# Laying the narrow projection columns of an attention layer out by kind, in one wide product per token block

## The chip, the cores and the metric

The kernel runs on one NeuronCore of a Trainium2 chip. The metric is the device time of one execution in microseconds; lower is better. Kernels are compared by the median of several executions.

## The reference

The reference runs three network blocks one behind the other on a sequence of 256 tokens with 1024 features, in 32-bit floats. The change is in the third block, a hybrid layer. There one input projection `h = x @ w_in` gives the operands of four mixers. Cut to what matters:

```
h = x @ w_in
(q_n, kc, vc, ks, vs, kw, vw, g_n, q_m, k_m, v_m, conv_in, q_h, f_h, i_h, g_h) = jnp.split(h, split_points, axis=-1)
gates = jax.nn.sigmoid(g_n.reshape(B, S, NSA_HEADS, 3))
o_nsa = nsa_attention(q_n, kc, vc, ks, vs, kw, vw, gates, rel_tab[:NSA_HEADS])
```

For the NSA attention q_n has 256 columns; the keys and values of its three branches, kc and vc (compressed), ks and vs (selected), kw and vw (window), have 64 columns each, shared by the four heads; and g_n has 12 columns, three gates for each of four heads. q_m, k_m and v_m, 256 columns each, belong to the second attention (MoBA).

## The kernel before

**Weights.** All large weights reach the core as 440 units of 128 x 2048 floats (1 MB), laid out on the host by `lay_unit`, in the order in which TensorE asks for them (`unit`). For a 1024-row weight a unit holds 256 columns of eight row tiles (j = 0 to 7). SyncE's queue loads unit n into a ring of three buffers, as soon as unit n - 3 has been split (`sp_weights`, L323). ScalarE makes the high part of it (`hi`, L118, the tile `weights_hi`), VectorE the rest (`lo`, L313, `weights_lo`), both into two buffers in turn. So `hi` of unit n waits for its transfer and for TensorE to have finished unit n - 2, `lo` waits for `hi`, and TensorE's first matmul of the unit waits for `lo`. The numbers of the units follow from the program, and each engine's order is the order in which its own function calls `hi`, `lo`, the copies and the matmuls.

**Products.** Every product is made of three matmuls in fp32r, high by high and the two mixed ones (`mm3`, L105): 24 matmuls for the 1024 rows. In a feature-major product (`pe_tile`) the weights are the stationary operand and the 256 tokens move (256 columns); the result has features on its partitions. In a token-major product (`pe_tokens`, `pe_tile_tok`) 128 tokens are stationary and the weights move, as many columns as there are features. In the trace the form `128*64 128x256` is a stationary operand of 64 columns and 256 moving ones, `128*128 128x12` one of 128 columns and 12 moving ones. Results stand in PSUM banks; before it writes a bank, TensorE waits in `empty` for the copies out of it that were named when the bank was last taken.

**The stage.** `pe_attention3` runs these products in a row: the NSA queries (Q_N, unit 0 of this count); a unit of 256 columns from KV_C on, which holds kc, vc, ks and vs; a unit from KV_W on, which holds kw, vw, the gates, and columns that nobody reads there; and then the projections Q_M, K_M, V_M, CONV_A and CONV_G, a unit each, 48 matmuls of 256 columns each (two tiles). Out of the two NSA units TensorE makes

- kc and vc together, one feature-major tile of 24 matmuls (bank 2),
- ks, 24 matmuls with 64 stationary columns (bank 3, `pe_keys`),
- vs, a token-major product for each block of 128 tokens, 2 x 24 matmuls of 64 columns (banks 0 and 1, `pe_tokens`),
- kw, as ks (bank 2); vw, as vs (banks 0 and 1),
- the gates, 2 x 24 matmuls of 12 columns (banks 2 and 3).

ScalarE's `act_attention3` copies the compressed pair (`cmp_tokens`, four copies, waits `kv_c`), each value product (`v_sel_win`) and applies the sigmoid to the gates (`nsa_gates`, L2990, waits `nsa_tokens`), with two calls of `hi` among them. VectorE's `dve_attention3` copies the two key products (`k_sel_win`, L3027 and L3030) between calls of `lo`. All of Q_M's, K_M's and later tiles go into banks 0 and 1 in turn (a projection takes both banks before its first matmul), and ScalarE and VectorE share the copies out of them (L435, L488).

Behind the projections, `pe_mixers`, `act_mixers`, `dve_mixers` and GpSimd's `pool_attention3` run the attentions, a 31-tap convolution and a recurrent mixer. The NSA part of it reads `k_sel_win`, `v_sel_win` and `nsa_gates`.

The semaphore of a signal is found by its kind (`TOGETHER`, L20 on): the kinds of one list share one semaphore, and the values are counted in program order.

Of the kernel before, what the change touches and what calls it, by code (L numbers as in the profile page):

```python
# [12 lines left out]
P = 128  # L13
# [20 lines left out]
    "scalar_attention": ("dup", "nsa_took", "cmp_exp", "cmp_by_key", "cmp_hid", "conv_silu"),  # L34
# [291 lines left out]
def empty(k, pe, b, *marks):  # L326

    for m in k.emptied[b]:
        pe.wait_ge(*k.s.at(*m))
    k.emptied[b] = marks  # L330
    return k.bank[b]
# [2450 lines left out]

MOBA = ("moba",)
# [3 lines left out]
def pe_tokens(k, pe, ap, at, width, b, bank, n):  # L2787
    out = empty(k, pe, bank, ("nsa_took", n))[:, 0:width]
    for j in range(KT):
        i = mm3(pe, out, k.x[:, j, b * P:(b + 1) * P], ap[:, j, at:at + width], j == 0, j == KT - 1)  # L2790
    i.then_inc(*k.s.up("nsa_tokens", n))


def pe_keys(k, pe, ap, at, bank, n):
    out = empty(k, pe, bank, ("k_sw", n))[0:64, 0:S]
    for j in range(KT):
        i = mm3(pe, out, ap[:, j, at:at + 64], k.x[:, j, :], j == 0, j == KT - 1)
    i.then_inc(*k.s.up("nsa_keys", n))
# [6 lines left out]
def pe_attention3(k, pe):  # L2805
    pe_project(k, pe, ("qn",), [w3(Q_N)], took_both(("qn",)), split_mark(("in3",)))
    ap = unit(k, pe, *w3(KV_C))
    out = empty(k, pe, 2, ("dup", 1, 1))[:, 0:S]
    pe_tile(k, pe, ap, 0, k.x, out).then_inc(*k.s.up("kv_c"))
    pe_keys(k, pe, ap, 128, 3, 0)  # L2810
    for b in range(NB):
        pe_tokens(k, pe, ap, 192, 64, b, b, b)
    unit_done(k, "nsa_tokens", 1)
    ap = unit(k, pe, *w3(KV_W))
    pe_keys(k, pe, ap, 0, 2, 1)
    for b in range(NB):
        pe_tokens(k, pe, ap, 64, 64, b, b, 2 + b)
    for b in range(NB):
        pe_tokens(k, pe, ap, 128, 12, b, 2 + b, 4 + b)
    unit_done(k, "nsa_tokens", 5)  # L2820
# [22 lines left out]
def pe_nsa_scores(k, pe, n):  # L2843
# [3 lines left out]
        bias_call(k, 2 * pair + hd, qb)], True, (("nsa_took", 5), ("k_sw", 1)))  # L2847
# [123 lines left out]
def act_attention3(k, act):  # L2971
# [13 lines left out]
    for n, (b, dst) in enumerate(((0, k.v_sw[:, 0, 0, :]), (1, k.v_sw[:, 1, 0, :]), (0, k.v_sw[:, 0, 1, :]),  # L2985
                                  (1, k.v_sw[:, 1, 1, :]), (2, k.gates[:, 0, :]), (3, k.gates[:, 1, :]))):
        if n == 2:
            hi(k, act)
        act.wait_ge(*k.s.at("nsa_tokens", n))
        act.activation(dst, k.bank[b][:, 0:12 if n >= 4 else 64], ACT.Sigmoid if n >= 4 else ACT.Copy) \  # L2990
            .then_inc(*k.s.up("nsa_took", n))
# [912 lines left out]
```

## Time and profile before

| | us |
|---|---|
| median of 3 runs | 3101.13 |
| lowest, highest run | 3089.43, 3102.24 |
| span of the profiled execution (first to last instruction) | 3091.2 |
| TensorE's matmuls busy | 2956.2 (96%) |
| VectorE busy, ScalarE busy, GpSimd busy | 1719.5 (56%), 1434.4 (46%), 166.1 (5%) |
| mean granted TensorE clock over the span (1.00 is 2.4 GHz) | 0.976 |
| moved by DMA | 492.89 MB, mean 159 GB/s |

The profile gives its execution's span and no separate time for it; the span lies 1.8 us above the lowest of the three runs and 9.9 us below their median. The profile is read in this way: the busy shares tell which engine has least room; the chain that ended last follows the end of the program back from one releaser to the next; the waits name who held whom up; the timeline gives each instruction's start and length; and the table of stretches gives, for any stretch, each engine's busy time and the clock that TensorE was granted in it. Matmuls overlap in the timeline, so their pace is the distance between two starts and not the length of one.

### The profile page before, as it was taken

The page shows a single profiled execution, that of the slowest core. Times are in us where ns is not written, and L with a number is a line of the kernel's source. Part 1 is how long each engine was busy: PE and PEld are TensorE (multiplying, and loading weights), DVE is VectorE, ACT ScalarE, POOL GpSimd, SP SyncE. Part 2 cuts the span into 40 slices and gives each one's busy share as a digit, 9 for nine tenths or more (in the row PEclk, how much of TensorE's full clock was granted, in tenths as well). Part 3 has the DMA queues.
Part 4 walks back from the last instruction along what each step waited for, and adds up shares of the span by engine and source line. Part 5 has one row for each costly group of instructions (what it writes and reads, how often), then busy time and mean ns, then how long its engine had stood idle before and what let it go on. Part 6 is the DMA issues. An engine that isn't in the chain of part 4 may idle for free.

```text
span 3091.2 us, 53947 instructions
## 1 busy us (share of the span) xinstructions
PE 2956.2 (96%) x23720; PEld 2748.8 (89%) x23720; DVE 1719.5 (56%) x2029; ACT 1434.4 (46%) x1831; POOL 166.1 (5%) x197
## 2 busy tenths in 40 slices
PE   8999998999999998999999999999979999999998
PEld 8988898999998998999989899899869899886887
DVE  5454555545464555545555654555786554465555
ACT  4455655445455655444445444444541344344444
POOL 1000100000000110001000000000011000045000
PEclk9999999999999999999999999999989999889999
DMA  6553334554543334556454455555320255441453
GB/s 249 185 189 124 137 137 153 188 191 177 184 180 128 138 141 158 185 185 230 180 204 165 154 186 186 179 181 191 138 82 4 73 189 185 151 152 54 152 179 134
DMA packets 69394, 492.89 MB, mean 159 GB/s; under 512 B 7853, under 2 KB 9421, under 8 KB 10534
## 3 DMA queue, kind: packets, MB, share of 16 engines
q1 hardware_dynamic: 64224, 465.53, 41.7%
q10 hardware_dynamic: 4938, 23.92, 2.0%
q8 instruction: 188, 3.08, 0.4%
q14 instruction: 44, 0.36, 0.0%
HBM read 488.32 MB, written 1.06 MB: 158 GB/s over the span
## 4 chain that ended last, share of the span: by engine, by line
PE 84%; DVE 8%; ACT 5%; issue 2%; PEld 0%; DMA 0%; POOL 0%; ACTq 0%; PEldq 0%; DVEq 0%; SPq 0%; POOLq 0%
PE bank L105 54%; PE acc L105 29%; ACT weights_hi L118 2%; DVE weights_lo L313 2%; DVE tmp L673 1%; DVE h L666 1%; DVE h L681 1%; PEld acc L105 0%; DVE b_x_lo L505 0%; PE acc L1005 0%; DMA weight_ring<-in_weights 0%; DVE b_x_lo L733 0%; ACT tmp L1084 0%; ACT L1084 0%; ACT b_x_hi L118 0%
## 5 line engine op out<-in xcount | busy, mean ns | idle before, releaser
L313 DVE TENSOR_TENSOR weights_lo<-weight_ring,weights_hi 128x2048 fp32r<-128x2048 f32 x440 | 1010.7, 2297 | 933.8 <-ACT weights_hi L118 933.3
L105 PE MATMUL bank<-b_x_hi,weights_hi 128*128 128x256 f32 x3576 | 1015.2, 284 | 15.6 <-DVE b_x_lo L733 10.6
L118 ACT ACTIVATE weights_hi<-weight_ring 128x2048 fp32r<-128x2048 f32 x440 | 839.6, 1908 | 370.6 <-PE acc L105 355.4
L105 PE MATMUL bank<-b_x_hi,weights_lo 128*128 128x256 f32 x3576 | 1009.6, 282 | 0.0
L105 PE MATMUL bank<-b_x_lo,weights_hi 128*128 128x256 f32 x3576 | 1008.3, 282 | 0.0
L105 PEld LDWEIGHTS bank<-b_x_hi,weights_hi 128*128 128x128 f32 x3576 | 677.3, 189 | 28.5 <-issue 13.3
L105 PEld LDWEIGHTS bank<-b_x_lo,weights_hi 128*128 128x128 f32 x3576 | 677.8, 190 | 3.4
L105 PEld LDWEIGHTS bank<-b_x_hi,weights_lo 128*128 128x128 f32 x3576 | 676.6, 189 | 0.0
L105 PE MATMUL acc<-weights_hi,b_hidden_hi 128*128 128x512 f32 x832 | 329.7, 396 | 0.0
L105 PE MATMUL acc<-weights_hi,b_hidden_lo 128*128 128x512 f32 x832 | 328.2, 394 | 0.0
L105 PE MATMUL acc<-weights_lo,b_hidden_hi 128*128 128x512 f32 x832 | 327.3, 393 | 0.0
L118 ACT ACTIVATE b_hidden_hi<-act_gate 128x256 fp32r<-128x256 f32 x208 | 86.9, 418 | 341.2 <-DVE act_gate L890 313.6
L866 ACT ACTIVATE act_gate<-bank 128x256 f32<-128x256 f32 x176 | 67.6, 386 | 276.0 <-PE bank L105 275.9
L105 PEld LDWEIGHTS acc<-weights_hi,b_hidden_lo 128*128 128x128 f32 x832 | 156.5, 188 | 37.9
L105 PEld LDWEIGHTS acc<-weights_lo,b_hidden_hi 128*128 128x128 f32 x832 | 156.7, 188 | 32.7
L105 PEld LDWEIGHTS acc<-weights_hi,b_hidden_hi 128*128 128x128 f32 x832 | 156.5, 188 | 32.5 <-DVE weights_lo L313 0.4
L105 PE MATMUL bank<-weights_hi,b_x_hi 128*128 128x256 f32 (+2 forms) x528 | 154.3, 292 | 9.3 <-DVE weights_lo L313 7.6
L105 PE MATMUL bank<-weights_lo,b_x_hi 128*128 128x256 f32 (+2 forms) x528 | 153.8, 291 | 0.0
L105 PE MATMUL bank<-weights_hi,b_x_lo 128*128 128x256 f32 (+2 forms) x528 | 153.8, 291 | 0.0
L105 PE MATMUL acc<-b_x_hi,weights_hi 128*128 128x256 f32 x416 | 125.4, 301 | 15.5 <-ACT tmp L1084 10.3
L893 DVE TENSOR_TENSOR b_hidden_lo<-act_gate,b_hidden_hi 128x256 fp32r<-128x256 f32 x176 | 75.3, 428 | 85.2 <-ACT b_hidden_hi L118 85.2
L105 PE MATMUL acc<-b_x_hi,weights_lo 128*128 128x256 f32 x416 | 121.5, 292 | 0.0
(487 smaller groups left out, 3999.6 us busy)
## 6 DMA issues: line engine op xcount, KB each, us to landing
weight_ring<-in_weights SPq DMA_DIRECT2D x440, 1024.0 KB, 4.8
xn<-in_norm_rows ACTq DMA_DIRECT2D x14, 1024.0 KB, 4.7
sgu_bias_row<-in_sgu_rows ACTq DMA_DIRECT2D x1, 2048.0 KB, 10.9
sgu_norm_rows<-in_sgu_rows ACTq DMA_DIRECT2D x1, 2048.0 KB, 9.6
bias_hankel<-bias_scratch ACTq DMA_DIRECT2D x1, 1536.0 KB, 6.2
h<-in_x SPq DMA_DIRECT2D x2, 512.0 KB, 6.6
mem_norm<-in_memory SPq DMA_DIRECT2D x1, 1024.0 KB, 13.8
sgu_w_spatial<-in_sgu_w_spatial ACTq DMA_DIRECT2D x1, 1024.0 KB, 4.7
```

Of the source, the lines that this page charges most:

```text
L105: return pe.matmul(out, a, b, start=start, stop=stop, skip_group_check=True)
L118: return act.activation(out, in_, ACT.Copy, scale=scale)
L313: dve.tensor_tensor(k.w.lo[:, n % 2, :], k.ring[:, n % RING, :], k.w.hi[:, n % 2, :], ALU.subtract) \
L666: dve.scalar_tensor_tensor(out=h, in0=h, scalar=alpha / scale, in1=acc_of(k, b), op0=ALU.mult, op1=ALU.add, accum_out=stat(k, 0, b)).then_ ...
L673: dve.scalar_tensor_tensor(out=k.t[:, b], in0=k.h[:, b, :], scalar=stat(k, 1, b), in1=k.rows[:, 0], op0=ALU.add, op1=ALU.mult).then_inc(*k ...
L681: dve.scalar_tensor_tensor(out=half(k.h[:, b], i), in0=half(k.t[:, b], i), scalar=stat(k, 6, b), in1=half(k.rows[:, 1], i), op0=ALU.mult, ...
L866: act.activation(k.act_gate[:, c, :], k.bank[c][:, 0:S], ACT.Silu).then_inc(*k.s.up("silu", f, j, c))
L893: dve.tensor_tensor(k.hid.lo[:, j % 2, c, :], k.act_gate[:, c, :], k.hid.hi[:, j % 2, c, :], ALU.subtract) \
```

## The change

The columns of the two NSA units are laid out anew. The first unit (`FEATURE_PARTS`) holds kc, vc, ks, kw, all that is wanted feature-major: TensorE makes two tiles of 128 features from it, the compressed pair in bank 2 and both keys in bank 3. The second (`TOKEN_PARTS`) holds vs, vw and the gates, 64 + 64 + 12 = 140 columns: one token-major product of 140 columns for each block of tokens, block 0 in bank 0 and block 1 in bank 1. `lay_unit` puts the columns together on the host. The number of units stays at 440.

```diff
-    "scalar_attention": ("dup", "nsa_took", "cmp_exp", "cmp_by_key", "cmp_hid", "conv_silu"),
+    "scalar_attention": ("dup", "v_sw", "gates", "cmp_exp", "cmp_by_key", "cmp_hid", "conv_silu"),
...
+def w3_parts(*parts):
+
+    return ("parts", "w_in_3", 0, parts)
+
+
+FEATURE_PARTS = w3_parts((KV_C, 128), (KV_S, 64), (KV_W, 64))
+TOKEN_PARTS = w3_parts((KV_S + 64, 64), (KV_W + 64, 76))
+TOKENS_W = 140
...
-def pe_tokens(k, pe, ap, at, width, b, bank, n):
-    out = empty(k, pe, bank, ("nsa_took", n))[:, 0:width]
+def pe_tokens(k, pe, ap, b):
+    out = empty(k, pe, b, ("gates", b))[:, 0:TOKENS_W]
     for j in range(KT):
-        i = mm3(pe, out, k.x[:, j, b * P:(b + 1) * P], ap[:, j, at:at + width], j == 0, j == KT - 1)
-    i.then_inc(*k.s.up("nsa_tokens", n))
-
-
-def pe_keys(k, pe, ap, at, bank, n):
-    out = empty(k, pe, bank, ("k_sw", n))[0:64, 0:S]
-    for j in range(KT):
-        i = mm3(pe, out, ap[:, j, at:at + 64], k.x[:, j, :], j == 0, j == KT - 1)
-    i.then_inc(*k.s.up("nsa_keys", n))
+        i = mm3(pe, out, k.x[:, j, b * P:(b + 1) * P], ap[:, j, 0:TOKENS_W], j == 0, j == KT - 1)
+    i.then_inc(*k.s.up("nsa_tokens", b))
...
 def pe_attention3(k, pe):
     pe_project(k, pe, ("qn",), [w3(Q_N)], took_both(("qn",)), split_mark(("in3",)))
-    ap = unit(k, pe, *w3(KV_C))
-    out = empty(k, pe, 2, ("dup", 1, 1))[:, 0:S]
-    pe_tile(k, pe, ap, 0, k.x, out).then_inc(*k.s.up("kv_c"))
-    pe_keys(k, pe, ap, 128, 3, 0)
+    ap = unit(k, pe, *FEATURE_PARTS)
+    pe_tile(k, pe, ap, 0, k.x, empty(k, pe, 2, ("dup", 1, 1))[:, 0:S]).then_inc(*k.s.up("kv_c"))
+    pe_tile(k, pe, ap, 1, k.x, empty(k, pe, 3, ("k_sw", 1))[:, 0:S]).then_inc(*k.s.up("nsa_keys"))
+    unit_done(k, "nsa_keys")
+    ap = unit(k, pe, *TOKEN_PARTS)
     for b in range(NB):
-        pe_tokens(k, pe, ap, 192, 64, b, b, b)
+        pe_tokens(k, pe, ap, b)
     unit_done(k, "nsa_tokens", 1)
-    ap = unit(k, pe, *w3(KV_W))
-    pe_keys(k, pe, ap, 0, 2, 1)
-    for b in range(NB):
-        pe_tokens(k, pe, ap, 64, 64, b, b, 2 + b)
-    for b in range(NB):
-        pe_tokens(k, pe, ap, 128, 12, b, 2 + b, 4 + b)
-    unit_done(k, "nsa_tokens", 5)
...
-    for n, (b, dst) in enumerate(((0, k.v_sw[:, 0, 0, :]), (1, k.v_sw[:, 1, 0, :]), (0, k.v_sw[:, 0, 1, :]),
-                                  (1, k.v_sw[:, 1, 1, :]), (2, k.gates[:, 0, :]), (3, k.gates[:, 1, :]))):
-        if n == 2:
-            hi(k, act)
-        act.wait_ge(*k.s.at("nsa_tokens", n))
-        act.activation(dst, k.bank[b][:, 0:12 if n >= 4 else 64], ACT.Sigmoid if n >= 4 else ACT.Copy) \
-            .then_inc(*k.s.up("nsa_took", n))
+    hi(k, act)
+    for b in range(NB):
+        act.wait_ge(*k.s.at("nsa_tokens", b))
+        copy_act(act, flat2(k.v_sw[:, b, :, :]), k.bank[b][:, 0:P]).then_inc(*k.s.up("v_sw", b))
+        act.activation(k.gates[:, b, :], k.bank[b][:, P:TOKENS_W], ACT.Sigmoid).then_inc(*k.s.up("gates", b))
...
-    dve.wait_ge(*k.s.at("nsa_keys", 0))
-    dve.tensor_copy(k.k_sw[:, 0, :], k.bank[3][0:64, 0:S]).then_inc(*k.s.up("k_sw", 0))
+    dve.wait_ge(*k.s.at("nsa_keys"))
+    for e in range(2):
+        dve.tensor_copy(k.k_sw[:, e, :], k.bank[3][64 * e:64 * e + 64, 0:S]).then_inc(*k.s.up("k_sw", e))
     lo(k, dve)
-    dve.wait_ge(*k.s.at("nsa_keys", 1))
-    dve.tensor_copy(k.k_sw[:, 1, :], k.bank[2][0:64, 0:S]).then_inc(*k.s.up("k_sw", 1))
```

The two waits of the NSA scores on `nsa_took` 5 (TensorE in `pe_nsa_scores`, VectorE in `dve_mixers`) become waits on `gates` 1, and `lay_unit` learns the kind "parts", which joins the named column ranges.

On TensorE the place is the end of the NSA products and the first matmuls of Q_M (in brackets the semaphores that a row waits for: `s_w_lo` is that of the unit's low part, `s_scalar_attention` that of ScalarE's copies out of the banks). Before:

```order
L105 MATMUL bank3<-weights_hi,b3_x_hi 128x12
L105 MATMUL bank3<-weights_lo,b3_x_hi 128x12
L105 MATMUL bank3<-weights_hi,b3_x_lo 128x12
L105 MATMUL bank0<-b3_x_hi,weights_hi 128x256 [waits s_scalar_attention,s_w_lo]
L105 MATMUL bank0<-b3_x_lo,weights_hi 128x256
L105 MATMUL bank0<-b3_x_hi,weights_lo 128x256
```

With the change:

```order
L105 MATMUL bank1<-weights_hi,b3_x_hi 128x140
L105 MATMUL bank1<-weights_lo,b3_x_hi 128x140
L105 MATMUL bank1<-weights_hi,b3_x_lo 128x140
L105 MATMUL bank0<-b3_x_hi,weights_hi 128x256 [waits s_scalar_attention,s_w_lo]
L105 MATMUL bank0<-b3_x_lo,weights_hi 128x256
L105 MATMUL bank0<-b3_x_hi,weights_lo 128x256
```

Q_M's first matmul stands 120 matmuls earlier. Its wait on ScalarE is for the copies out of banks 0 and 1: before, those of the value products, with 48 gate matmuls since; now those of the product that has just ended.

On ScalarE the place is the same stage, between the copies of the compressed pair and Q_M's:

```order
 L118 ACTIVATE cmp_tokens<-bank 64x256 x4
-L2990 ACTIVATE v_sel_win<-bank 128x64 x2
-L118 ACTIVATE weights_hi<-weight_ring 128x2048
-L2990 ACTIVATE v_sel_win<-bank 128x64 x2
-L2990 ACT_TABLE_LOAD
-L2990 ACTIVATE nsa_gates<-bank 128x12 x2
+L118 ACTIVATE weights_hi<-weight_ring 128x2048
+L118 ACTIVATE v_sel_win<-bank 128x128
+L2986 ACT_TABLE_LOAD
+L2986 ACTIVATE nsa_gates<-bank 128x12
+L118 ACTIVATE v_sel_win<-bank 128x128
+L2986 ACTIVATE nsa_gates<-bank 128x12
```

Q_M's high part moves ahead of all value copies, the table load stands between the first copy and the first sigmoid, and the copy and the sigmoid of the second block stand behind the last matmul of the stage.

## Rows read from the trace of the kernel before

**Rows 1.** The page: busy shares, and the chain that ended last by engine

```profile
PE 2956.2 (96%) x23720; PEld 2748.8 (89%) x23720; DVE 1719.5 (56%) x2029; ACT 1434.4 (46%) x1831; POOL 166.1 (5%) x197
...
PE 84%; DVE 8%; ACT 5%; issue 2%; PEld 0%; DMA 0%; POOL 0%; ACTq 0%; PEldq 0%; DVEq 0%; SPq 0%; POOLq 0%
```

**Rows 2.** Stretches of the stage: length, busy by engine, clock, DMA share, GB/s

```profile
2675.88:2678.72 2.84, 2.84 (x26) 2.84 (x25) 1.05 (x3) 2.38 (x3) 0.00 (x0) 1.00 0.58 237
2678.72:2681.52 2.80, 2.80 (x26) 2.80 (x25) 1.86 (x1) 1.52 (x4) 0.00 (x0) 1.00 0.03 6
2681.52:2688.06 6.54, 6.54 (x50) 6.54 (x49) 0.42 (x1) 0.23 (x1) 0.00 (x0) 0.80 0.48 162
2688.06:2692.79 4.73, 4.73 (x26) 4.73 (x26) 2.29 (x1) 2.02 (x2) 0.00 (x0) 0.56 0.00 0
2692.79:2700.27 7.48, 7.48 (x51) 7.48 (x49) 0.42 (x1) 0.22 (x1) 0.00 (x0) 0.69 0.40 142
2700.27:2710.51 10.24, 10.24 (x50) 10.24 (x50) 0.00 (x0) 1.69 (x3) 0.00 (x0) 0.50 0.00 0
2710.51:2719.64 9.13, 8.46 (x49) 8.28 (x50) 3.35 (x5) 2.99 (x5) 0.00 (x0) 0.69 0.35 115
```

**Rows 3.** Timeline of TensorE in the first 64-column products: start, length, instruction

```profile
2681.40 0.28 PE L105 MATMUL bank<-b_x_hi,weights_lo 128*64 128x256 f32 x1
2681.52 0.20 PE L105 MATMUL bank<-weights_hi,b_x_hi 128*128 128x64 f32 x1
2681.55 0.28 PE L105 MATMUL bank<-weights_lo,b_x_hi 128*128 128x64 f32 x1
...
2685.34 0.34 PE L105 MATMUL bank<-weights_hi,b_x_lo 128*128 128x64 f32 x1
2685.50 0.40 PE L105 MATMUL bank<-weights_hi,b_x_hi 128*128 128x64 f32 x1
```

**Rows 4.** Timeline of TensorE, first and last matmul of Q_M, first of K_M

```profile
2710.51 0.56 PE L105 MATMUL bank<-b_x_hi,weights_hi 128*128 128x256 f32 x1
...
2718.70 0.28 PE L105 MATMUL bank<-b_x_hi,weights_lo 128*128 128x256 f32 x1
2719.64 0.36 PE L105 MATMUL bank<-b_x_hi,weights_hi 128*128 128x256 f32 x1 [0.67 <-DVE q_moba L488]
```

**Rows 5.** Timeline of ScalarE between the key and the query products

```profile
2678.92 1.59 ACT L118 ACTIVATE cmp_tokens<-bank 64x256 f32<-64x256 f32 x4 [0.66 <-PE bank L105]
2684.32 0.23 ACT L2990 ACTIVATE v_sel_win<-bank 128x64 f32<-128x64 f32 x1 [3.81 <-PE bank L105]
...
2700.73 1.28 ACT L2990 ACT_TABLE_LOAD   x1
...
2710.69 0.18 ACT L2990 ACTIVATE nsa_gates<-bank 128x12 f32<-128x12 f32 x1 [4.94 <-PE bank L105]
2710.77 1.90 ACT L118 ACTIVATE weights_hi<-weight_ring 128x2048 fp32r<-128x2048 f32 x1
```

**Rows 6.** ScalarE's copy of 128x256 out of a bank

```profile
L435 ACT ACTIVATE v_moba<-bank x1: 384/384/384, 2731.3 to 2731.3; 128x256 f32<-128x256 f32 x1
```

**Rows 7.** Timeline of VectorE in the same stage

```profile
2678.29 2.29 DVE L313 TENSOR_TENSOR weights_lo<-weight_ring,weights_hi 128x2048 fp32r<-128x2048 f32 x1 [1.79 <-ACT weights_hi L118]
2681.72 0.42 DVE L3027 COPY k_sel_win<-bank 64x256 f32<-64x256 f32 x1 [1.14 <-PE bank L105]
```

**Rows 8.** Weight ring from 2655 to 2740 us: count of transfers and their landing

```profile
L323 SPq DMA_DIRECT2D weight_ring<-in_weights x8: 327/328/328, 2658.6 to 2736.7; - x8
...
DMA to landing us min/median/max: 4.7/4.9/6.6
```

**Rows 9.** Stretches elsewhere, columns as in Rows 2

```profile
221.00:224.00 3.00, 2.04 (x18) 1.84 (x16) 2.96 (x3) 2.18 (x3) 0.00 (x0) 1.00 0.01 3
224.00:228.00 4.00, 3.37 (x28) 3.37 (x29) 3.39 (x4) 1.27 (x1) 0.00 (x0) 1.00 0.52 205
...
2740.00:2770.00 30.00, 30.00 (x207) 23.82 (x205) 24.86 (x42) 17.73 (x31) 22.22 (x17) 1.00 0.42 153
```

More of the change, by code:

```diff
@@ L2846, in pe_nsa_scores @@
         (k.qn[:, 2 * pair + hd, qb * P:(qb + 1) * P], k.k_sw[:, kind, 0:(qb + 1) * P]),
-        bias_call(k, 2 * pair + hd, qb)], True, (("nsa_took", 5), ("k_sw", 1)))
+        bias_call(k, 2 * pair + hd, qb)], True, (("gates", 1), ("k_sw", 1)))
 def pe_compress(k, pe, e, half):
@@ L3539, in dve_mixers @@
     lo(k, dve)
-    dve.wait_ge(*k.s.at("nsa_took", 5))
+    dve.wait_ge(*k.s.at("gates", 1))
     dve_max(k, dve, ("nsa", 0), 0)
@@ L3765, in lay_unit @@
     w = inputs[name][index]
-    if kind == "rows":
+    if kind == "parts":
+        part = np.concatenate([w[:, at:at + n] for at, n in start], axis=1)
+    elif kind == "rows":
         part = w[start:start + 256]
```

## The prediction

> **What bounds the kernel now.** I read the page first. TensorE has matmuls running in 96% of the span, and 84% of the chain that ended last is its own work [rows 1]. So time is saved where TensorE gets less to do or does it faster, and a step on another engine counts only if TensorE comes to wait for it.
>
> Next I cut the stage of the change into stretches at the first matmul of each product [rows 2]. In order they are the compressed pair (24 matmuls, 2.84 us), the selected keys (24, 2.80), the selected values (48 of 64 columns, 6.54), the window keys (24, 4.73), the window values (48 of 64, 7.48), the gates (48 of 12 columns, 10.24), and Q_M up to the first matmul of K_M (48, 9.13). From the selected keys to K_M's start that is 40.92 us, with TensorE busy for 40.25 of them. The reader is to see two things. A product with 12 columns costs no less than one with 256. And the clock is at 1.00 (2.4 GHz) in the first two rows, at 0.50 (1.2 GHz) in the gates, and between them in the others, although TensorE has no idle time from the selected keys to the gates.
>
> The timeline shows why narrow products are dear. At full clock the 64-column matmuls from 2681.55 to 2685.34 start 34 steps apart, 0.1115 us each [rows 3]; those with 256 columns take 2.84 / 24 = 0.118 [rows 2]. At half clock the step is 10.24 / 48 = 0.213 with 12 columns [rows 2]. The step thus hardly depends on the moving columns; the 128-column weight load that each matmul brings is the likely floor. The clock fell at about 2685.4, after 3.9 us of 64-column products [rows 3]; it was back within the window keys, fell again in the window values, and came back only inside Q_M.
>
> **The change on TensorE.** It takes out 216 matmuls and puts in 96: 120 fewer.
>
> - Keys. The second tile of the new feature unit replaces both key products. It is a full 128 x 256 tile, as the compressed pair is: 2.84 us [rows 2] for 2.80 + 4.73 = 7.53. Gain 4.69.
> - Values and gates. 48 matmuls of 140 columns replace 144, which took 6.54 + 7.48 + 10.24 = 24.26 us. No row has 140 columns, so the step is bounded by the nearest ones: 0.1115 (64 columns) below, 0.118 (256) above. I take 0.1115, because the stationary operand is the same, and because 64 columns stream in no more than 0.03 us (the second 64-column matmul starts that soon behind the first [rows 3]), so 140 should in about 0.065, below the step. To the start of the last matmul that makes 47 x 0.1115 = 5.24 us (5.55 by the upper end).
> - The wait that is new. Q_M takes banks 0 and 1. Before, they had been copied out while the gates ran; now bank 1 holds the product that has just ended, so the copy and the sigmoid are exposed. The pattern stands at the other end of Q_M: from its last matmul to K_M's first 0.94 us pass, with one copy of 0.43 in it (idle 0.67, released by that copy) [rows 4]. Here ScalarE has a copy of 128 x 128 and a sigmoid of 128 x 12 in its place. The sigmoid took 0.18 [rows 5], the copy lies between 0.23 for 64 columns [rows 5] and 0.38 for 256 [rows 6]; I take 0.28. So 0.94 - 0.43 + 0.28 + 0.18 = 0.97 us from the last narrow matmul to Q_M's first (0.92 to 1.07). The table load of 1.28 us [rows 5] stands behind the first block's copy, under the 24 matmuls (2.7 us) of the second block: 0.28 + 1.28 + 0.18 = 1.74, covered by 0.9. If it were not, up to 1.3 us would be added.
> - Q_M itself. Before it began at half clock and took 9.13 us to K_M's first matmul. If the clock stays up in front of it, it takes 47 x 0.118 + 0.94 = 6.50. Gain 2.63, not from fewer matmuls but from the clock.
>
> Sum after: 2.84 + 5.24 + 0.97 + 6.50 = 15.55 us for 40.92. **Gain 25.4 us.** At full clock throughout, the old stage would have taken 2 x 2.80 + 3 x 5.35 + 6.50 = 28.2 us (5.35 is 48 x 0.1115), so half of the gain, 12.8, is the clock, and 12.6 the 120 matmuls less the new wait.
>
> On the clock the Trainium skill (TensorE: Matmul & The Clock Gate, "The HAM clock gate") says that it follows how busy the array is and that gaps between bursts throttle it. The trace agrees only in part: here it fell with TensorE's matmuls back to back and no gap. By the page, 140-column products without a gap hold the clock, which is the forecast; by the trace that has to be weighed, below. The same page ("Back-to-back issue gap") gives about 81 ns per pair of load and matmul at 128 columns; by that the 140-column product would take 3.8 us and the gain would be 26.8. The trace has 0.1115 for even fewer columns, and that decides.
>
> **The other engines and queues.** The weight supply has to follow a faster TensorE.
>
> - The token unit. Its high part is made as before, its low part from 2678.29 to 2680.58 [rows 7]; TensorE will want it at 2678.72 + 2.84 = 2681.6. Margin 1.0 us, where it was 7.5.
> - Q_M's unit. Its `hi` is queued on ScalarE ahead of the value copies, and waits for the keys' last matmul. Then 1.90 [rows 5] and 2.29 [rows 7] make 4.2, plus about 0.2 of hand-overs, under 5.24 + 0.97 of TensorE. ScalarE is free again 1.9 us after the keys, and the first block ends 2.7 us after them: nothing behind that `hi` is late. VectorE's two key copies (0.42 each [rows 7]) stand ahead of `lo`, but within the 1.90 us in which it waits for `hi`.
> - K_M's unit. Its `hi` starts behind the last sigmoid, with 4.4 us to go for 6.5.
> - The ring. SyncE's queue has the same 440 transfers. In this stage 8 of them landed in 4.7 to 6.6 us [rows 8]. Each may take two units' time, 11 us or more, as in the full-clock stretches. Cost nothing; the cover is that prefetch.
> - ScalarE has two operations fewer, VectorE has the same two copies; neither is on the path but for the new wait.
>
> What is late next is again TensorE, in the bank hand-overs of 0.9 us between projections. All behind them is released relative to Q_M's start, so the gain should reach the end whole.
>
> **The number.** The sum is made in the profiled execution: span 3091.2 - 25.4 = 3065.8 us. Against the median of the three runs, 3101.13, which lies 9.9 us above that span, it gives 3075.7 us, 0.8% less. About 0.5% (15.5 us) is what a measurement of this kernel can tell from no change; the three runs alone spread over 12.8.
>
> **Rivals.**
>
> - *The clock falls in the 140-column product too.* For it: 64 columns back to back did not hold it [rows 3]. Against it: a stretch in which matmuls of 256 columns ran for only 2.04 us out of 3.00 and then waited kept 1.00, and so did what followed [rows 9]; the new product has no such hole. 140 columns lie between these rows, nearer the 256 by ratio. Price: falling as late as the 64-column one did, the second block runs at 0.213, 24 x 0.102 = 2.4 us, and Q_M begins at half clock as before, 2.6; all 48 at half clock, 4.9 + 2.6. Gain 18 to 20.4, time about 3082. A short fall through the new pause alone costs some 1.5 us and belongs to the forecast.
> - *The step grows with the columns below 256.* If the 0.1115 of 64 columns were set by these and not by the load, 140 would take 0.244: 6.4 us more, gain 19.0, time 3082. Against it: the 0.03 us in which 64 columns streamed [rows 3], and 12 columns at half clock were no faster than the load.
> - *The units come late.* The margin of 1.0 us at the token unit, or a transfer that is slow because 3 MB are fetched in half the time, makes TensorE wait. To bring the gain below 15.5 us it has to lose 9.9; a transfer would have to land some 10 us later than the slowest of the eight [rows 8]. Time 3086 to 3097.
> - *Slower than before: the clock stays down through the mixers.* If the new pause, or the shifted places of the later pauses, left TensorE at half clock, each 256-column matmul would take 0.095 us more. After 267 of them (57 us) the gain is gone; the projections and the next unit are 288. With 430, up to the middle of the mixers, the kernel is 15.5 us slower, 3117. Against it: full clock came back inside Q_M with the same kind of stream, and the 30 us from 2740 on are at 1.00 with attention steps in between [rows 9].
>
> **Chances.** Forecast 0.76, clock falls 0.11, step by columns 0.06, late units 0.05, slower 0.02. The first gives faster by over 0.5% in 93 of 100 measurements (the gain is 10 us above the bound, the runs scatter by up to 6 each way), the next two in about 70, late units none. Faster 0.76 x 0.93 + 0.17 x 0.7 = 0.83, slower 0.02, within 0.5% 0.15. The range holds the forecast with the spread of the runs below (3101.13 - 25.4 - 12), and above the two rivals at 3082 with 7 us of spread: 3064 to 3089.
>
> **What would show it.** In the changed kernel: 96 matmuls between Q_N and Q_M, 48 of them with 140 columns at steps of 0.11 to 0.12; granted clock 1.00 from the compressed pair to the end of Q_M; one idle time of TensorE of 0.7 to 0.95 us in front of Q_M, released by ScalarE's `nsa_gates`; no idle time in front of the 140-column product; 15 to 16 us from the second feature tile to K_M. Steps of 0.21, or 0.24, would name the first or second rival, a wait on `weights_lo` the third, a clock below 1.00 in the projections behind the fourth. If the stage gains 25 us and the span does not, the forecast is wrong in that the gain reaches the end.

## The result and the profile after

| | kernel before | changed kernel |
|---|---|---|
| median, beside the first comparison (4 runs each) | 3100.32 | 3076.78 |
| lowest and highest of these | 3089.43 to 3102.24 | 3064.85 to 3077.64 |
| median, second comparison (11 and 6 runs) | 3100.04 | 3075.63 |
| span of the profiled execution | 3091.2 | 3075.8 |

The ratio of the times is 0.9921 with a 95% interval of 0.9901 to 0.9941, and 0.9924 [0.9912, 0.9936] in the second comparison. Forecast were 3075.7 us and a range of 3064 to 3089; the time is 1.1 us above the forecast, faster by more than 0.5%.

On the page of the changed kernel (busy shares, the clock in 40 slices, the chain that ended last), which answers to [rows 1]:

```profile
PE 2941.0 (96%) x23600; PEld 2732.3 (89%) x23600; DVE 1718.2 (56%) x2029; ACT 1436.3 (47%) x1829; POOL 166.3 (5%) x197
...
PEclk9999999999999999999999999999979999998999
...
PE 84%; DVE 8%; ACT 5%; issue 2%; PEld 0%; DMA 0%; POOL 0%; PEldq 0%; ACTq 0%; DVEq 0%; SPq 0%; POOLq 0%
```

TensorE has 120 matmuls fewer and bounds the kernel as before. The stage itself, in three stretches cut at the first matmul of the second feature tile, of the 140-column products and of Q_M (columns as in [rows 2]; the first three columns behind the stretch are its length, TensorE's matmuls and its weight loads, and the clock follows GpSimd):

```profile
2686.50:2689.36 2.86, 2.86 (x27) 2.86 (x25) 1.86 (x1) 1.52 (x4) 0.00 (x0) 1.00 0.13 26
2689.36:2695.36 6.00, 5.47 (x50) 5.35 (x49) 3.13 (x3) 4.15 (x7) 0.00 (x0) 1.00 0.57 186
2695.36:2701.97 6.61, 5.93 (x49) 5.76 (x49) 3.27 (x5) 2.68 (x4) 0.00 (x0) 1.00 0.52 207
```

Together 15.47 us, where the five stretches from the selected keys to K_M's start took 40.92 in [rows 2]. The clock is at 1.00 (2.4 GHz) in all three; in [rows 2] it went down to 0.50. TensorE's timeline shows the steps, in the form of [rows 3] and [rows 4]:

```profile
2689.36 0.23 PE L105 MATMUL bank<-weights_hi,b_x_hi 128*128 128x140 f32 x1
2689.42 0.27 PE L105 MATMUL bank<-weights_lo,b_x_hi 128*128 128x140 f32 x1
...
2694.56 0.27 PE L105 MATMUL bank<-weights_hi,b_x_lo 128*128 128x140 f32 x1
2695.36 0.36 PE L105 MATMUL bank<-b_x_hi,weights_hi 128*128 128x256 f32 x1 [0.53 <-ACT nsa_gates L2986]
```

From the second to the last narrow matmul (2689.42 to 2694.56) 46 steps pass, 0.1117 us each; then 0.80 us to Q_M's first. ScalarE's timeline, in the place of [rows 5], shows what TensorE waits for there:

```profile
2692.19 0.28 ACT L118 ACTIVATE v_sel_win<-bank 128x128 f32<-128x128 f32 x1 [0.66 <-PE bank L105]
2692.49 1.28 ACT L2986 ACT_TABLE_LOAD   x1
2693.78 0.18 ACT L2986 ACTIVATE nsa_gates<-bank 128x12 f32<-128x12 f32 x1
2694.87 0.28 ACT L118 ACTIVATE v_sel_win<-bank 128x128 f32<-128x128 f32 x1 [0.91 <-PE bank L105]
2695.05 0.18 ACT L2986 ACTIVATE nsa_gates<-bank 128x12 f32<-128x12 f32 x1
```

The table load lies wholly under the second block's matmuls. In the last two rows the sigmoid starts 0.18 us behind the copy's start, not 0.28: the two overlap by 0.10.

**Where the rest is.** The stage gained 25.45 us, the two profiled spans differ by only 15.4. The other 10 are not in the change: both executions run the same instructions ahead of it, and there the changed one was 7.6 us later (the high part of the first unit that the change touches was begun on ScalarE at 2676.72 instead of 2669.13). One stretch of RWKV and its neighbours holds nearly all of that. Kernel before, between two weight units:

```profile
2197.58:2478.02 280.44, 253.81 (x4127) 235.57 (x4126) 184.60 (x279) 100.45 (x152) 25.31 (x17) 0.94 0.21 73
```

Changed kernel, between the same two units:

```profile
2199.02:2486.64 287.62, 262.39 (x4127) 243.21 (x4126) 184.62 (x279) 100.97 (x153) 25.26 (x17) 0.91 0.21 73
```

The same 4127 matmuls, 7.2 us more, and a clock of 0.91 instead of 0.94; it is the 7 in the clock's slices above, where the page of before has an 8. Behind the stage it is another 2.3 us. Here and below that part is counted from the start of V_M's weight unit on ScalarE, which falls together with K_M's first products, to the end of the span (the expectations call it the stage's last unit, or its token unit): 371.9 before, 374.2 after. Over the 14 profiled executions of this study the start of that first touched unit lies between 2666.1 and 2677.9 us, and for one and the same kernel (tokens alone, below) at 2668.4 and 2673.0. The profiled execution of the kernel before was also one of its quicker ones: in every run that has both numbers the time is 1.8 us above the span, so its 3091.2 stands for some 3093, 7 us below the median, while the changed kernel's (3077.64) is 0.9 above its own. So a single pair of spans cannot show a gain of 25 us to better than some 10. The medians, 23.5 and 24.4 us apart, show it better; their intervals still leave 18 to 31 us and 20 to 27 us.

### The profile page after: what moved, and what is told of

The parts are those of the page before. It is cut to its first block, busy times and chain, and to the rows that moved or that the text cites. A ratio compares the mean times of both kernels' runs of the same rounds, so it can differ in the third digit from the quotient of the medians.

```text
span 3075.8 us, 53704 instructions
## 1 busy us (share of the span) xinstructions
PE 2941.0 (96%) x23600; PEld 2732.3 (89%) x23600; DVE 1718.2 (56%) x2029; ACT 1436.3 (47%) x1829; POOL 166.3 (5%) x197
## 4 chain that ended last, share of the span: by engine, by line
PE 84%; DVE 8%; ACT 5%; issue 2%; PEld 0%; DMA 0%; POOL 0%; PEldq 0%; ACTq 0%; DVEq 0%; SPq 0%; POOLq 0%
PE bank L105 53%; PE acc L105 29%; DVE weights_lo L313 2%; ACT weights_hi L118 2%; DVE tmp L673 1%; DVE h L666 1%; DVE h L681 1%; PEld acc L105 0%; DVE b_x_lo L505 0%; PE acc L1005 0%; DMA weight_ring<-in_weights 0%; DVE b_x_lo L733 0%; DVE tmp L613 0%; ACT tmp L1084 0%; ACT b_x_hi L118 0%
## 5 line engine op out<-in xcount | busy, mean ns | idle before, releaser
L105 PE MATMUL bank<-weights_hi,b_x_hi 128*128 128x256 f32 (+1 forms) x496 | 143.1, 289 | 8.9 <-DVE weights_lo L313 7.7
L105 PE MATMUL bank<-weights_lo,b_x_hi 128*128 128x256 f32 (+1 forms) x496 | 142.4, 287 | 0.0
L105 PE MATMUL bank<-weights_hi,b_x_lo 128*128 128x256 f32 (+1 forms) x496 | 142.1, 286 | 0.0
## 6 DMA issues: line engine op xcount, KB each, us to landing
mem_norm<-in_memory SPq DMA_DIRECT2D x1, 1024.0 KB, 14.2
```

What stands on the lines that cost most here:

```text
L105: return pe.matmul(out, a, b, start=start, stop=stop, skip_group_check=True)
```

## Experiments

### Old instructions, only wider: the clock by itself

The kernel before, its 144 narrow matmuls each moving 256 columns instead of 64 or 12. The number and order of the matmuls, the waits, and the number and width of the copies stay; the copies read their 64 or 12 columns where these now stand in the bank.

```
-    out = empty(k, pe, bank, ("nsa_took", n))[:, 0:width]
+    out = empty(k, pe, bank, ("nsa_took", n))[:, 0:256]
...
-        ... ap[:, j, at:at + width], ...
+        ... ap[:, j, 0:256], ...
```

> The kernel before, but each of its six narrow token-major products moves all 256 columns of the unit; the copies take the columns they want. As many matmuls as before, more columns. My theory (half of the gain is the clock, and a step costs a weight load whatever the columns): the clock stays at 1.00 from the keys to the end of the MoBA queries; the stage from the selected keys to the first matmul of the MoBA keys takes 2 x 2.80 + 144 x 0.118 + 6.5 = 29.1 us instead of 40.92, so this kernel is about 12 us faster than the one before (ratio 0.996). Rival (the number of matmuls and their columns set the time, and the clock fell by chance of the place): the stage takes 41 us or more, ratio 1.000 or above.

Measured: 3084.86 us median of 5 runs against 3098.86 of 9, ratio 0.9952 [0.9939, 0.9966]. The stage in stretches (selected keys; selected values; window keys; window values and gates; Q_M up to K_M):

```profile
2686.15:2688.95 2.80, 2.80 (x27) 2.80 (x25) 1.86 (x1) 1.51 (x4) 0.00 (x0) 1.00 0.07 21
2688.95:2694.64 5.69, 5.69 (x51) 5.69 (x49) 0.42 (x1) 0.22 (x1) 0.00 (x0) 1.00 0.49 186
2694.64:2697.43 2.79, 2.79 (x26) 2.79 (x25) 0.53 (x1) 2.03 (x2) 0.00 (x0) 1.00 0.00 0
2697.43:2708.83 11.40, 11.40 (x98) 11.40 (x97) 2.09 (x2) 1.91 (x4) 0.00 (x0) 1.00 0.27 93
2708.83:2715.38 6.55, 5.88 (x51) 5.70 (x49) 3.37 (x5) 3.02 (x5) 0.00 (x0) 1.00 0.12 21
```

29.2 us instead of 40.92, as expected, with four to twenty-one times as many columns moved in each of these matmuls and not one matmul fewer. The half clock is gone from every row. So narrow moving operands are what took the clock away, and that alone was worth 11.7 us here. The fewer matmuls of the real change bring the rest.

### Each half of the change alone

First the keys alone: the new feature unit and its full second tile, and behind it the old six products of 64, 64 and 12 columns out of the token unit (their six copies on ScalarE come back too).

```
     unit_done(k, "nsa_keys")
     ap = unit(k, pe, *TOKEN_PARTS)
-    for b in range(NB):
-        pe_tokens(k, pe, ap, b)
+    for n, (at, w) in enumerate(((0, 64), (64, 64), (128, 12))):
+        for b in range(NB):
+            pe_tokens(k, pe, ap, at, w, b, 2 * (n == 2) + b, 2 * n + b)
```

> Only the keys' part of the change: both keys in one full tile; values and gates stay narrow products (64, 64 and 12 columns for each block), out of the token unit. Theory by parts added up: 4.7 us less than before, stage 36.2 us. Theory with the clock: the second key product is gone that brought the clock back between the value products, so 34 of the 144 narrow steps run at 0.1115 and 110 at 0.213, 27.2 us, and the MoBA queries begin at half clock, 9.1: stage 39 us (38 to 40), only 1.5 to 2 less than before.

One execution: 3097.2 us. Its stretches (key tile; 96 matmuls of 64 columns; 48 of 12; Q_M up to K_M):

```profile
2678.93:2681.79 2.86, 2.86 (x26) 2.86 (x25) 1.87 (x1) 1.52 (x4) 0.00 (x0) 1.00 0.03 9
2681.79:2698.12 16.33, 16.33 (x98) 16.33 (x97) 3.13 (x3) 2.58 (x4) 0.00 (x0) 0.63 0.37 128
2698.12:2708.36 10.24, 10.24 (x49) 10.24 (x50) 0.00 (x0) 1.69 (x3) 0.00 (x0) 0.50 0.01 2
2708.36:2717.26 8.90, 8.23 (x50) 8.05 (x50) 3.36 (x5) 2.99 (x5) 0.00 (x0) 0.71 0.36 118
```

38.33 us, inside the 38 to 40 of the theory with the clock and not the 36.2 of the parts added up. As a difference of rows the prediction's 4.69 for the keys was right (7.53 became 2.86), but 1.9 of it is the low clock of the window keys; the keys alone bring 2.6. The window keys had brought the clock back between two narrow products; without them the 96 products of 64 columns run at 0.63 on average.

Then the tokens alone: the 140-column product, with the keys as two products of 64 rows.

```
-    pe_tile(k, pe, ap, 1, k.x, empty(k, pe, 3, ("k_sw", 1))[:, 0:S]).then_inc(*k.s.up("nsa_keys"))
+    for n in range(2):
+        out = empty(k, pe, 3 if n == 0 else 2, ("k_sw", n))[0:64, 0:S]
+        for j in range(KT):
+            i = mm3(pe, out, ap[:, j, 128 + 64 * n:192 + 64 * n], k.x[:, j, :], j == 0, j == KT - 1)
+        i.then_inc(*k.s.up("nsa_keys", n))
```

> Only the tokens' part: one product of 140 columns for each block, but the two keys as two products with 64 stationary columns, 24 matmuls each. Expected: clock 1.00 throughout; stage as in the changed kernel (15.47 us) with 2 x 2.80 for the keys instead of 2.86: 18.2 us. If the gain of the parts did not depend on the clock, it would be 20.2 (15.47 + 4.7).

(VectorE's two key copies follow.) One execution: 3079.54 us. From the first key product to K_M 18.22 us, as expected (2678.125 to 2696.342): keys 5.60, tokens with the new pause 6.01, Q_M 6.61. The last two stretches:

```profile
2683.72:2689.73 6.01, 5.48 (x50) 5.36 (x49) 2.71 (x2) 4.15 (x7) 0.00 (x0) 1.00 0.16 41
2689.73:2696.34 6.61, 5.94 (x48) 5.76 (x49) 3.35 (x5) 2.67 (x4) 0.00 (x0) 1.00 0.54 207
```

So the tokens alone are worth 22.7 of the 25.45 us, and the keys 2.75 on top of them. Merging the values and gates is the change; the key tile is a small addition.

### The step of a product, by its columns

Two variants of the changed kernel. In the first, the 140 columns are taken as 128 and then 12, so each block has 48 matmuls:

```
-    for j in range(KT):
-        i = mm3(pe, out, ..., ap[:, j, 0:TOKENS_W], j == 0, j == KT - 1)
+    for at, to in ((0, P), (P, TOKENS_W)):
+        for j in range(KT):
+            i = mm3(pe, out[:, at:to], ..., ap[:, j, at:to], at + j == 0, j == KT - 1)
```

> The changed kernel with each 140-column product cut into one of 128 and one of 12 columns, in the same bank: 48 matmuls more. If the step is the weight load whatever the columns, and the clock holds, the token products take 96 x 0.1115 = 10.7 us instead of 5.2, at 12 columns as at 128. If the step followed the columns, the 12-column ones would take next to nothing, and the token products stay near 5.5 us. If the clock falls in the 12-column ones, their steps are 0.213 from there on, and the MoBA queries begin below full clock.

One execution: 3095.53 us. Stretches (128 columns and 12 of the first block, 128 and 12 of the second, Q_M up to K_M):

```profile
2687.19:2689.81 2.62, 2.62 (x26) 2.62 (x25) 1.26 (x3) 1.91 (x1) 0.00 (x0) 1.00 0.88 306
2689.81:2693.39 3.58, 3.58 (x27) 3.58 (x26) 1.88 (x1) 0.00 (x0) 0.00 (x0) 0.73 0.45 108
2693.39:2698.55 5.16, 5.16 (x26) 5.16 (x26) 0.00 (x0) 1.74 (x3) 0.00 (x0) 0.50 0.42 178
2698.55:2704.30 5.75, 5.22 (x25) 5.16 (x26) 0.00 (x0) 0.49 (x3) 0.00 (x0) 0.50 0.00 0
2704.30:2712.79 8.49, 7.82 (x49) 7.65 (x49) 3.35 (x5) 2.67 (x4) 0.00 (x0) 0.75 0.34 125
```

and TensorE's timeline at the change from 128 to 12 columns, still at full clock:

```profile
2689.81 0.22 PE L105 MATMUL bank<-weights_hi,b_x_hi 128*128 128x12 f32 x1
2689.90 0.25 PE L105 MATMUL bank<-weights_lo,b_x_hi 128*128 128x12 f32 x1
...
2691.24 0.25 PE L105 MATMUL bank<-weights_lo,b_x_hi 128*128 128x12 f32 x1
```

From 2689.90 to 2691.24 there are 12 steps of 0.112 us with 12 columns; with 128 columns the step is 2.62 / 24 = 0.109, at half clock 5.16 / 24 = 0.215. 12, 64, 128 and 140 columns cost the same. But 48 more matmuls of 12 columns cost not only their 5.4 us: the clock falls during the first 24, and the 128-column products behind them run at half clock too. The span from the token product to K_M is 25.6 us against 12.6.

In the second, the product moves 256 columns, 116 of them padding that nobody reads.

> The changed kernel with the token products 256 columns wide instead of 140 (116 columns of padding more, never read). If the step of a product is set by more than its columns, as the 0.1117 us at 140 and the 0.118 us at 256 columns say, 47 steps cost 0.3 us more and the stage is 15.7 to 15.9 us. If columns set it, 47 steps would grow by 256/140 to 9.6 us and the stage be 19.8. The clock stays at 1.00 in the stage in either case.

Stretches (the 256-column token product with its pause; Q_M up to K_M):

```profile
2678.62:2685.00 6.38, 5.85 (x50) 5.68 (x49) 3.13 (x3) 4.15 (x7) 0.00 (x0) 1.00 0.60 187
2685.00:2691.61 6.61, 5.94 (x48) 5.76 (x49) 3.26 (x5) 2.67 (x4) 0.00 (x0) 1.00 0.58 196
```

0.38 us more than with 140 columns. The one execution took 3064.58 us; that it is below the changed kernel's median is not the wider product but mostly the part ahead: the first touched unit was begun at 2666.1, the earliest of all and some 10 us before the changed kernel's. Another 2.4 to 2.7 us came behind the stage (371.5 against 373.9 and 374.2).

### What is left of the stage: the bank hand-overs

Q_M, K_M, CONV_A and CONV_G each take over both banks just after they were filled, and TensorE waits for the last copy out of them. (V_M takes its banks one at a time and shows no wait.) The first two waits stand above; the other two, in the second execution of the changed kernel:

```profile
2713.34 0.36 PE L105 MATMUL bank<-b_x_hi,weights_hi 128*128 128x256 f32 x1 [0.56 <-ACT v_moba L435]
2719.88 0.36 PE L105 MATMUL bank<-b_x_hi,weights_hi 128*128 128x256 f32 x1 [0.61 <-DVE conv_in L3035]
```

First only the token products are moved to banks 2 and 3:

```
-    out = empty(k, pe, b, ("gates", b))[:, 0:TOKENS_W]
+    out = empty(k, pe, 2 + b, ("gates", b))[:, 0:TOKENS_W]
```

> The changed kernel with the token products in banks 2 and 3, nothing else: only the pause ahead of Q_M's first tile goes, and the three behind it stay. Theory (a pause costs its own length): stage 14.8 to 15.0 us instead of 15.5, median 0.5 to 1 us below the changed kernel, under what three rounds can tell. Rival (each pause also costs clock later, since the four together gave 9 us in the medians where they measure 2.4): 2 us or more below the changed kernel.

3074.62 us median of 4 runs (3067.8, 3070.4, 3078.8, 3080.9), ratio to the kernel before 0.9935 [0.9913, 0.9958]. The token stretch falls from 6.00 to 5.31 us, the stage to 14.79, as expected. The pause is gone and gives 0.69 us, somewhat more than its idle time of 0.53: from the last narrow matmul's start to Q_M's first it had been 0.80 us, and is now 0.11, one step. In the time of the whole 0.7 us cannot show: the four runs lie in two pairs ten microseconds apart, and the changed kernel was not run beside them. So whether a pause also costs clock later, the rival, stays open here.

Then K_M's and CONV_A's tiles also go to banks 2 and 3, so that neighbours alternate throughout (the copies follow):

```
+SHIFT = {("km",): 2, ("conv_a",): 2}
+def bank_of(of, t):
+    return (t + SHIFT.get(of, 0)) % 4
...
-        outs = [empty(k, pe, t % 4, *taken(t))[:, 0:S] for t in (2 * n, 2 * n + 1)]
+        outs = [empty(k, pe, bank_of(of, t), *taken(t))[:, 0:S] for t in (2 * n, 2 * n + 1)]
```

> The token products go to banks 2 and 3 and K_M's and CONV_A's tiles to banks 2 and 3 too, so that no tile follows another into a bank that was just filled. In the changed kernel TensorE paused 0.53 us ahead of Q_M's first tile, and before Q_M's, K_M's and CONV_A's neighbours the kernel before showed pauses of 0.56 to 0.67 us. Theory (the pauses are what is left of the stage, and nothing else is waited for there): the stage is 14.8 us to Q_M's side plus the removed pause of 0.6 at K_M, 14.2 to 14.4 us in all instead of 15.5, and with the pauses behind K_M the whole is 2 to 3 us shorter than the changed kernel, ratio to it about 0.9992, near what five rounds can tell. Rival (the pauses are filled by a weight wait behind them: the ring lands Q_M's unit too late): stage 15.3 or more, a wait named on weights_lo or weights_hi in place of that on the evacuation.

3066.61 us median of 5 runs, ratio to the kernel before 0.9902 [0.9888, 0.9916], beside 0.9924 [0.9912, 0.9936] for the changed kernel on the same chip. Key tile, tokens and Q_M:

```profile
2687.07:2689.91 2.84, 2.84 (x27) 2.84 (x25) 1.85 (x1) 1.52 (x4) 0.00 (x0) 1.00 0.03 3
2689.91:2695.22 5.31, 5.31 (x50) 5.31 (x49) 3.14 (x3) 3.65 (x4) 0.00 (x0) 1.00 0.57 201
2695.22:2700.96 5.74, 5.74 (x51) 5.74 (x50) 2.63 (x2) 2.53 (x4) 0.00 (x0) 1.00 0.56 193
```

The stage is 13.89 us, 1.6 below the changed kernel's and below the 14.2 expected, and none of the pauses is left among TensorE's waits. No weight unit comes late in their place: the rival is out. In the kernels that have them the four measure 0.53 + 0.67 + 0.56 + 0.61 = 2.4 us of idle time. What they cost is more: from the first token matmul to the end of CONV_G it is 34.0 us without them (2689.91 to 2723.91) and 37.2 with them (2688.54 to 2725.75), 3.2 us. The medians differ by 9.0, more than the 2 to 3 expected, yet the two intervals overlap, so how much of that is real stays open. In the profiled executions the part behind the stage went from 373.9 to 367.8 us, with 26.8 us at half clock instead of 33.8: some 3.5 us of it would be that.

### A wait in the mixers that some executions meet

The two experiments with 381.7 and 381.3 us behind the stage (tokens alone, and gates apart) had one thing in common: in the mixers TensorE reached the convolution's mean before GpSimd's last tap. To test it, that one step is moved in TensorE's order, behind the scores of head pair 3:

```
-    pe_conv_sum(k, pe, k.conv, ("mean", CONV), ...)
     pe_nsa_values(k, pe, ("nsa", 0), 0, 0)
     pe_nsa_scores(k, pe, 3)
+    pe_conv_sum(k, pe, k.conv, ("mean", CONV), ...)
```

It was made in the changed kernel first, then on top of the banks:

> The changed kernel once more, on the chip and beside the runs of the kernel before that the next three share. The stage from the first selected-key or pair product to the first K_M product should again take 15.5 us (between 15.3 and 15.7), wherever the span ends. The span itself may move by ten microseconds: the theory of the scatter is that in some executions TensorE reaches the convolution's mean before GpSimd's taps are done, waits about 0.9 us and then has the half clock for some 20 us, which costs about 10. If that theory holds, an execution of about 3075 us shows no wait on conv_out ahead of the mean, and one of about 3080 or more, if it is longer behind the stage, shows one.

> The changed kernel with one step of TensorE's order moved: the convolution's mean stands behind the scores of head pair 3 instead of ahead of the values of head pair 0. Theory (a wait for GpSimd's taps there, then 20 us at the half clock, makes the longer executions): the profiled execution shows no wait on conv_out ahead of the mean, and the stretch from the stage's token unit to the end is 372 to 375 us, never 378 or more; the median is up to 4 us below the changed kernel's if its executions fall on both sides, and equal where they mostly don't meet the wait. Rival (the wait is a symptom; the clock falls for another reason, the share of TensorE's work in that stretch): the half-clock stretch of about 20 us comes back in some executions without any wait ahead of it, and medians agree within 1 us. Second rival: VectorE, which centres after the mean, is now late for the maxima of head pair 3, and the time is up by 3 to 6 us.

> Both edits together. If they are independent, their gains against the changed kernel add: 2 to 3 us for the pauses, and 0 to 4 for the mean. If removing the pauses only brings TensorE earlier to GpSimd's taps (theory of the scatter), no_handover alone gives back part of its gain and this one does not: this one is then 3 us or more below no_handover.

The changed kernel again gave 3075.63 us (stage 15.46), with the mean later 3072.07 (6 runs, ratio 0.9916 [0.9901, 0.993]), with banks and mean 3070.43 (5 runs, 0.9907 [0.9895, 0.992]). For the theory these decide nothing: neither of the changed kernel's two profiled executions met the wait, so there was nothing to remove, and both are within each other's intervals. But they are a control: the move by itself leaves the part behind the stage as it was (374.2 us, beside 374.2 and 373.9). On top of the banks the step gains nothing (3070.43 against 3066.61), contrary to the expectation. In the kernel without pauses GpSimd's last tap came sooner too, 95.8 us after the start of V_M's weight unit, and TensorE at 97.4 did not have to wait for it.

The kernel with the tokens alone does meet it, so the step was tried there:

> The kernel of the token-products-only experiment again. Its stage should again be 18.2 us. Its one execution before had TensorE waiting 0.9 us for GpSimd's taps ahead of the convolution's mean and then 20.5 us at the half clock, and 381.7 us from the stage's last unit to the end against 371.9 to 374.2 in kernels without that wait. Theory (the wait brings the half clock on): if the wait is there again the part behind is 380 to 383 us, if not 372 to 375. Rival (chance, unrelated to the wait): the two come apart.

> The same kernel with the convolution's mean behind the scores of head pair 3, so that TensorE can't wait for GpSimd's taps there. Theory (the wait brings the half clock on): no wait, no stretch of 20 us at half clock, the part behind the stage 372 to 375 us, and the median 5 to 9 us below the kernel it is made from, where that one meets the wait in most executions. Rival (the half clock has another cause): the part behind is 380 us or more in spite of the missing wait, and the medians agree within 2 us.

Without the move 3082.67 us median (4 runs, 3080.14 to 3085.2; ratio 0.9962 [0.9947, 0.9977]), with it 3075.35 (4 runs, 3073.32 to 3077.43; 0.9937 [0.992, 0.9953]): 7.3 us, and no run of one among those of the other. Without the move the wait is there again, in TensorE's timeline:

```profile
2798.47 0.60 PE L105 MATMUL acc<-conv_out,cons 128*128 128x256 f32 x2
2799.94 0.70 PE L105 MATMUL acc<-conv_out,cons 128*128 128x256 f32 x2 [0.87 <-POOL conv_out L3129]
```

in GpSimd's, the last tap that it waits for:

```profile
2799.08 0.81 POOL L3129 TENSOR_TENSOR conv_out<-conv_out,conv_gate 128x256 f32<-128x256 f32 x1
```

and its stretches around that place:

```profile
2790.00:2800.00 10.00, 9.13 (x36) 4.69 (x33) 4.43 (x10) 5.43 (x15) 8.98 (x11) 1.00 0.09 37
2800.00:2810.00 10.00, 10.00 (x28) 5.22 (x28) 5.04 (x15) 1.54 (x5) 2.38 (x3) 0.63 0.01 2
2810.00:2820.00 10.00, 10.00 (x37) 6.56 (x37) 4.08 (x17) 3.78 (x16) 0.00 (x0) 0.69 0.00 0
```

With the move, the same stretches:

```profile
2790.00:2800.00 10.00, 10.00 (x44) 5.55 (x42) 4.03 (x10) 4.53 (x11) 8.92 (x12) 1.00 0.07 28
2800.00:2810.00 10.00, 10.00 (x48) 6.28 (x46) 6.52 (x19) 2.74 (x13) 2.48 (x3) 1.00 0.01 2
2810.00:2820.00 10.00, 9.29 (x38) 5.55 (x37) 3.48 (x16) 5.88 (x20) 1.78 (x3) 0.83 0.00 0
```

The wait is 0.9 us, but behind it the clock is at 0.63 and 0.69 for 20 us, and without it at 1.00 and 0.83. The part behind the stage is 378.0 us with the wait (the expectation had 380 to 383, so it was 2 us too high) and 374.2 without (372 to 375 expected). So the profiled pair shows 3.8 us for the wait; the rest of the 7.3 in the medians is not in this pair and was not traced.

Counted from the start of V_M's weight unit, GpSimd's last tap starts at 98.0 to 98.4 us in the twelve profiled executions of kernels whose K_M and CONV_A stand in their old banks. TensorE came to the mean 97.5 to 97.8 us after that point in the four that waited (377.8 to 381.7 us behind the stage). It came at 98.2 to 99.9 in the six with the mean in its old place that did not wait (371.5 to 374.2, and 378.5 for the keys alone). In all four that waited a stretch of 10.2 or 20.5 us at half clock begins at 101.6 to 102.0; none of the other ten executions has any half clock between 92 and 111. Nor does the early arrival by itself bring it on: in the kernel without pauses TensorE came at 97.4, found the taps done and kept its clock there. So the half clock that begins there goes with the wait. It is not the only way to a long part behind the stage: the keys alone have 378.5 without waiting, with 10.2 us at half clock from 122.9 on. A TensorE that came up to 2.3 us sooner to that place ended 4 to 10 us later, as far as these executions show.

Of the bank experiment's two pairs of runs, the profiled run (3080.93) is one that waits. Whether the lower pair escapes the wait or was quicker ahead of the stage, no trace shows.

## Why the prediction was right

- **Keys, 2.84 us.** Measured 2.86. The gain of 4.69 booked for them is in part the clock's, as the keys alone showed.
- **Token product, 47 x 0.1115 = 5.24.** Measured 5.20; the second matmul started 0.06 us behind the first, as estimated, and the other 46 steps are 0.1117. The rival "step grows with the columns" is out: 12, 128 and 140 columns have the same step, 256 has 0.118.
- **New wait, 0.97 (0.92 to 1.07).** Measured 0.80, outside its bounds: the one term that was clearly mis-sized. The copy's 0.28 and the sigmoid's 0.18 were right, but were added end to end. Their starts are 0.18 apart, an overlap of 0.10. The Trainium skill (ScalarE: Activation LUTs, "What ACT_TABLE_LOAD costs") says that back-to-back activations overlap by about 93 ns; the rows agree. The remaining 0.07 is the hand-over, 0.51 taken from the other end of Q_M, here 0.44. There, in the kernel before, the copy that [rows 4] name is

```profile
2719.01 0.43 DVE L488 TENSOR_SCALAR q_moba<-bank 64x256 f32<-64x256 f32 x1 [2.57 <-PE bank L105]
```

From the last matmul's start to the start of the copy it is 0.31 us in both places; from the end of the last copy to TensorE's restart it was 0.20 there and is 0.13 behind the sigmoid. Why these differ was not tested.
- **Table load, hidden.** 2692.49 to 2693.77, under the second block.
- **Q_M, 6.50 from the clock alone.** Measured 6.61, at a clock of 1.00. The 0.11 more is mostly its first step, 0.20 us instead of 0.118 (0.16 with the token products in other banks, where no pause stands in front). It hides a part of the 0.17 by which the wait was put too high.
- **Clock.** Forecast to hold. It did: in all nine profiled executions with a 140-column product, that product took 5.3 us without its pause or 6.0 with it, which is full clock. The half of the gain that was ascribed to it (12.8) stands at 11.7 by the widened kernel, whose 144 wider matmuls pay 0.9 us for their columns; together that is 12.6. The Trainium skill (TensorE: Matmul & The Clock Gate, "The HAM clock gate") ties the clock to how busy the array is; the widened kernel, where only the columns per matmul changed, fits that reading. The section's remark on gaps between bursts covers none of this: the clock fell in the kernel before while TensorE's matmuls filled every one of the stretches from the selected keys to the gates.
- **Margin of the token unit, 1.0 us.** Its low part ran from 2686.06 for 2.29 us, to 2688.35, and was wanted at 2689.36: 1.01. In the changed kernel's timeline of VectorE:

```profile
2686.06 2.29 DVE L313 TENSOR_TENSOR weights_lo<-weight_ring,weights_hi 128x2048 fp32r<-128x2048 f32 x1 [1.79 <-ACT weights_hi L118]
```

- **Sum, 15.55.** Measured 15.47 and 15.46; gain 25.45 of 25.4 in the trace. "The gain should reach the end whole" fits the medians within two microseconds (24.4 and 23.5), but their intervals are 4 to 6 us wide to each side, and it could not be seen in one pair of spans. The mechanism was right; that the time came out only 1.1 us from the forecast is in part luck, since the three runs from which it started spread over 12.8 us. The prediction had the spread of the runs as a width of 12 us and did not ask where it comes from. Part of it comes from the clock in RWKV, part from the race between TensorE and GpSimd in the mixers, which a change of TensorE's pace ahead of them can tip either way. The rival in which the clock stays down in the mixers had the right place, with up to 10 us between the executions seen here; but the changed kernel's two profiled executions did not meet the wait that brings most of this on.

## What to carry over

Where each matmul brings its own 128-column stationary operand, as here, count matmuls and not moving columns: the step was the same from 12 to 140 columns, and 6% longer at 256. (That the weight load sets this step is the prediction's reading. No run varied the load at a fixed width, so it is not shown.) And look at the clock's column in the stretches *behind* a run of narrow products, since those pay too. Before the spans of two executions are compared, take out the stretches in which both run the same instructions.

## What was not expected of the hardware

- Products of 12 columns take the clock from what stands behind them, with TensorE busy throughout: the 128-column product between two of them ran at 0.50, and Q_M at 0.75.
- Making the narrow matmuls *wider* made the kernel 14.0 us faster (3084.86 against 3098.86).
- One wait of 0.9 us in the mixers is followed by 10 to 20 us at half clock. Taking it away gave 3.8 us in the profiled pair and 7.3 in the medians. Why the same stream holds the clock without the wait was not settled. What brings TensorE to that place at 97.5 in one execution and at 99.9 in another was not settled either; the executions that waited had 7 to 10 us at half clock between 57 and 92 us behind the start of V_M's unit, the changed kernel's two, which did not, had 13.7.
